# The first five of eight contraction chunks of an output projection, moved into a scan

## What is computed

```python
h = rms_norm(x, norm_mix_g[l])
p = h @ w_in[l]
...
o_att = memory_cross_attention(q, mem_n, w_mk[l], w_mv[l])
o_conv = conformer_conv(pc, conv_w[l], conv_b[l], conv_ln_g[l], conv_ln_b[l])
o_rwkv = rwkv7_bidirectional(pr, ...)
x = x + jnp.concatenate([o_att, o_conv, o_rwkv], axis=-1) @ w_out[l]
x = x + expert_choice_ffn(rms_norm(x, norm_ffn_g[l]), w_router[l], w_e_gate[l], w_e_up[l], w_e_down[l])
```

## Time and profile before

| what | us |
|---|---|
| median of 3 runs | 1869.56 |
| lowest and highest | 1868.42, 1872.74 |
| the profiled execution | 1867.28 |
| its span in the trace | 1865.3 |

### The profile page before, as it was taken

One profiled execution on the slowest core, in us unless ns is written; L12 is line 12 of the kernel. 1 busy time (PEld: TensorE's weight loads), 2 busy tenths in 40 slices (PEclk: granted clock), 3 DMA queues, 4 the chain that ended last, 5 costly groups with the idle time before them and its releaser, 6 DMA issues.

```text
span 1865.3 us, 25999 instructions
## 1 busy us (share of the span) xinstructions
PE 1476.8 (79%) x11135; PEld 844.7 (45%) x11135; DVE 418.2 (22%) x849; ACT 302.9 (16%) x671; POOL 118.1 (6%) x223
## 2 busy tenths in 40 slices
PE   6999988889896888888888859877857576765764
PEld 2845866768444443433433238666532132321311
DVE  1011225330016122212221253744330000000002
ACT  1101223540001111111111111432110010100100
POOL 3000022000000000000000002222000000000000
PEclk9999999898988899999999979887879898988988
DMA  9762362123484599999999962200329999999995
GB/s 352 163 257 81 114 245 96 46 90 113 180 297 158 227 428 429 428 428 428 431 428 428 396 246 92 83 3 3 138 100 412 429 428 429 428 429 428 429 428 231
DMA packets 86556, 512.05 MB, mean 275 GB/s; under 512 B 9783, under 2 KB 14168, under 8 KB 61910
## 3 DMA queue, kind: packets, MB, share of 16 engines
q1 hardware_dynamic: 82742, 501.95, 66.3%
q0 software_dynamic: 3744, 9.06, 2.1%
HBM read 506.10 MB, written 3.15 MB: 273 GB/s over the span
## 4 chain that ended last, share of the span: by engine, by line
PE 60%; DMA 24%; issue 6%; DVE 5%; ACT 3%; POOL 1%; SPq 1%; POOLq 0%; ACTq 0%; DVEq 0%; PEldq 0%
PE ps L1229 48%; DMA ring<-in_w_e_up 15%; DMA ring<-in_exp_w 7%; PE ps L1654 4%; PE ps L1828 3%; DMA ring<-in_ada_w 1%; DMA brow<-in_ada_b 1%; DVE arena L2457 1%; PE ps L1261 1%; PE ps L1639 1%; ACT arena L998 1%; DMA arena<-in_causal 1%; ACT arena L988 1%; DVE stats L2144 0%; PE ps L2097 0%
## 5 line engine op out<-in xcount | busy, mean ns | idle before, releaser
L1229 PE MATMUL ps<-ring,arena 128*32 128x512 f32 (+4 forms) x3572 | 481.8, 651 | 164.1 <-DMA ring<-in_w_e_up 92.1
L1229 PEld LDWEIGHTS ps<-ring,arena 128*32 128x32 f32 (+1 forms) x3572 | 137.0, 123 | 455.3 <-issue 387.1
L1229 PE MATMUL ps<-hTs,ring 128*128 128x256 f32 (+2 forms) x1120 | 250.7, 384 | 3.3 <-PE ps L1229 3.3
L1229 PEld LDWEIGHTS ps<-hTs,ring 128*128 128x128 f32 (+2 forms) x1120 | 211.5, 190 | 42.2 <-issue 11.1
L1229 PE MATMUL ps<-arena 128*128 (+5 forms) x576 | 140.1, 399 | 2.4 <-POOL arena L667 2.4
L1654 PE MATMUL ps<-arena 128*128 128x512 f32 x256 | 117.5, 601 | 29.0 <-DVE arena L2457 29.0
L1229 PEld LDWEIGHTS ps<-arena 128*128 128x128 f32 (+1 forms) x576 | 122.8, 292 | 19.7 <-issue 12.8
L1229 PE MATMUL ps<-ring,hTs 128*128 128x512 f32 (+2 forms) x288 | 103.7, 513 | 0.0
L1654 PEld LDWEIGHTS ps<-arena 128*128 128x128 f32 x256 | 46.0, 189 | 103.0 <-ACT arena L1000 57.1
L2457 DVE COPY arena<-ps 128x512 f32<-128x512 f32 x32 | 22.1, 692 | 251.6 <-PE ps L1229 251.6
L2744 DVE TENSOR_TENSOR arena<-arena,ps 64x512 f32<-64x512 f32 x16 | 11.0, 690 | 298.9 <-ACT arena L1184 298.9
(11 more groups left out here) (428 smaller groups left out, 1217.6 us busy)
## 6 DMA issues: line engine op xcount, KB each, us to landing
ring<-in_exp_w SPq DMA_DIRECT2D x96, 2048.0 KB, 18.8
ring<-in_w_e_gate SPq DMA_DIRECT2D x32, 2048.0 KB, 18.8
ring<-in_w_e_up SPq DMA_DIRECT2D x32, 2048.0 KB, 23.3
ring<-in_w_e_down SPq DMA_DIRECT2D x32, 2048.0 KB, 24.4
ring<-in_w_in SPq DMA_DIRECT2D x22, 2048.0 KB, 14.1
ring<-in_ada_w SPq DMA_DIRECT2D x12, 2048.0 KB, 12.8
ring<-in_w_out SPq DMA_DIRECT2D x4, 2048.0 KB, 12.1
ring<-in_w_br_hg SPq DMA_DIRECT2D x2, 2048.0 KB, 15.7
```

The lines of the kernel that those rows point to most:

```text
L1229: return nc.tensor.matmul(o, lhsT, rhs, start=start, stop=stop)
```

## The change

The products of chunks 0 to 4 are taken out of the tail and put in front of the levels of pair 1, into banks 1 and 2 of both directions. VectorE adds each of these four partial results to `x` within the levels, one in each level, after both transposes. `solved` of pair 1 waits until all four are added, since it writes the same banks. The Silu of the convolution moves between the pairs. In the tail only the products of chunks 5 to 7 remain, in the same four banks as before, and their four additions. No product is added or left out; four additions are.

```diff
@@ scalar engine, in the loop over pairs, behind the state copies
+                if p == 0:
+                    act.wait_ge(S("conv_normed"), 1)
+                    for c in range(3):
+                        ins = nc.scalar.activation(MIX[:, 2 + c, :], CV[:, c, :], ACT.Silu, bias=col(1, VB["cbb"] + c),
+                                                   scale=col(1, VB["cg"] + c))
+                    ins.then_inc(S("conv_ready"), 1)
...
@@ tensor engine, solved(p, d)
                 pe.wait_ge(S("prod_out"), 8 * p + 6 + d + 1)
+                if p:
+                    pe.wait_ge(S("early_out"), 4)
...
@@ tensor engine
+            wout2 = [tile("wout2") for _ in range(2)]
+
+            def early_out(i, t):
+                return dbank(t, 1 + i, 0, 512)
+
+            def project_early():
+
+                for i in range(2):
+                    is_out(pe, jM(f"O{i}"))
+                pe.wait_ge(S("conv_ready"), 1)
+                for d in range(2):
+                    pe.wait_ge(S("prod_out"), 14 + d + 1)
+                for i in range(2):
+                    for t in range(TT):
+                        for k in range(5):
+                            ins = mm(early_out(i, t), MIX[:, k, t * P:(t + 1) * P], slot(wout2[i], (8, 512))[:, k, :],
+                                     k == 0, k == 4)
+                        ins.then_inc(S("early_full"), 1)
...
                     pe.wait_ge(S("prod_out"), 8 * p + 2 + 2 * d + 2)
+                if p:
+                    project_early()
                 with pe.Fori(0, 4) as lev:
...
-            for i in range(2):
-                is_out(pe, jM(f"O{i}"))
-            project(0, 1)
             pe.wait_ge(S("gn_squares"), 1)
+            outs = [(wout2[i], [job("y2", 2 * i + t) for t in range(TT)]) for i in range(2)]
             block_sums("gn2", c3(3072))
-            pe.wait_ge(S("conv_ready"), 1)
-            project(1, 5)
             pe.wait_ge(S("mix_ready"), 1)
-            project(5, KC)
+            for n, js in outs:
+                for t, j in enumerate(js):
+                    for k in range(5, KC):
+                        ins = mm(bank(j), MIX[:, k, t * P:(t + 1) * P], slot(n, (8, 512))[:, k, :], k == 5, k == 7)
+                    fills(ins, j)
...
@@ vector engine, in the loop over levels
                         nc.vector.transpose(XT[d], X[d]).then_inc(S("lev_out"), 1)
+                    if p:
+                        i, t = lev // 2, lev % 2
+                        dve.wait_ge(S("early_full"), lev + 1)
+                        c = slice(512 * i, 512 * i + 512)
+                        tt(x[:, t, c], x[:, t, c], dbank(t, 1 + i, 0, 512), ALU.add).then_inc(S("early_out"), 1)
```

More of the change, by code:

```diff
@@ L2700, in _ @@
             say(tt(MIX[:, 5:8, :], YY, BON, ALU.add), "mix_ready")
+            dve.wait_ge(S("early_out"), 4)
             for i in range(4):
```

## The result

| | kernel before | changed kernel |
|---|---|---|
| median of 10 runs, us | 1869.77 | 1882.99 |
| lowest and highest | 1866.51, 1875.02 | 1878.67, 1889.95 |
| the profiled execution, and its span | 1867.28, 1865.3 | 1887.13, 1884.8 |

The ratio is 1.0069, with a 95% interval of 1.0052 to 1.0086: the change costs 12.9 us, 9.7 to 16.1. The runs of either kernel spread over 8 to 11 us, which is new: the three runs shown ahead of the prediction lay within 4.3.

A forecast was written before the change was run, and what follows sets the result against it. It took TensorE's chain to bound pair 1 of the scan and VectorE's chain to `mix_ready` to hold the tail. Scan +16.8 and tail -2.5 gave +14.3, so a median of 1883.9 us, range 1875.5 to 1889.

The forecast's parts named there:

- 17.3 for the long products: Pair 1 of the scan, before the levels: forty passes lie whole on TensorE's chain, adding 17.3 us.
- 3.8 for two gaps: Pair 1's levels: the instruction gaps of 1.34 and 2.47 us go, as packets arrive during the long passes; 3.8 us saved.
- 1.5 for the clock in the levels: Pair 1's levels: TensorE at full clock after 17 us of dense work; 1.5 us saved.
- 0.8 for three additions: Pair 1's levels: three additions on VectorE each delay the next level by 0.27 us; 0.8 us added.
- 1.3 for the fourth: End of pair 1's levels: `solved` waits for the fourth addition behind the second transpose; 1.3 us added.
- 2.7 for the packets behind the loop: `solved` to the steps: forty more pairs shift packet boundaries, so the steps begin at 19.9 against 16.7 us; 2.7 later.
- 0 for the Silu: Between the pairs: pair 1's copies end 2.3 us later, covered by an existing gap; 0, or 1.8 without that cover.
- -2.5 for the tail: Tail: ends 2.5 us earlier, with TensorE idle 9.5 us, then its first 5 us at half clock.
- the signs named: Trace marks expected, among them `y_done` near 1337, five or more gaps between `solved` and the steps, TensorE idle 9 us.
- The one by which packets run ahead: Scan: long products let packets run far ahead, the four later gaps vanish; 12.4 us less, 1871.5, no change; chance 0.06.
- The rival in which the packets cost nothing and the clock is kind: Scan and tail: no packet cost, 2.5 less in the tail, last steps up to 2.8 less; 1875.9; chance 0.17.
- The rival with a bad clock: Clock falls during the long products (1887.3), and also stays low for all tail passes (both 1895); chance 0.15.

The follow-up runs named there:

- the long products alone: Kernel before plus the twenty early products in front of pair 1's levels, results dropped, tail, Silu and additions unchanged; 1.0059, +11.0 us (7.1 to 15.0).
- twenty tiny products: Kernel before plus twenty 32x32 by 32x8 products, results dropped, where the change has its long ones; 0.9998, -0.4 us.
- sixty-four tiny products: Kernel before plus sixty-four 32x32 by 32x8 products (128 pairs, one packet), results dropped, ahead of pair 1's levels; 1.0031, +5.8 us.
- the Silu alone: Kernel before with only the Silu of the convolution moved between the pairs; 1.0007, +1.3 us (-1.9 to +4.5).
- the tail alone: Kernel before with the products of chunks 0 to 4 left out of the tail and computed nowhere else; 0.9985, -2.8 us (-5.8 to +0.4).
- the additions moved: Changed kernel with the first three additions made while TensorE runs the long products and the fourth in level 0; 1.0073 against the kernel before.
- chunk 0 early: Kernel before with only chunk 0's four products early, additions ahead of the levels and in level 0, Silu at its old place; 1.0008, +1.5 us.

## Why the prediction was right

It gave 1883.9 (1875.5 to 1889); the median is 1882.99, and the measured difference 12.9 against 14.3. The mechanism is shown by two kernels that take the change apart: the long products alone cost 11.0 in the scan (7.1 to 15.0), and taking them out of the tail gives back 2.8 (-0.4 to 5.8). The small terms are less sure, and that the sum came so close is in part luck: some were too large, one too small. Point by point:

- **17.3 for the long products**: 17.41, at full clock, in one piece. Shown by the trace and by the products alone (+11.0 net of what they buy back, where 14.7 was forecast).
- **3.8 for two gaps**: gone in the changed kernel; in the list of waits no gap over 0.2 lies between 1297.69 and 1309.
- **1.5 for the clock in the levels**: full clock in all four, each 2.9, and so in all five kernels with twenty long products; right. That it is they who keep the clock up is likely, but the levels at full clock differ without them too: one of four before, two of four behind twenty tiny products.
- **0.8 for three additions, 1.3 for the fourth**: 0.2 and 1.3. The first term was mis-sized: of a delay of 0.43 I took 0.15 as hidden, and it was nearly all.
- **2.7 for the packets behind the loop**: that the boundaries move is shown (twenty against sixty-four tiny products), the size was wrong: 0.9 in the one pair of traces at equal clock, and within what kernels with the same boundaries differ by. I had the second packet land 4.7 us behind `solved` with a wait; no wait stood there, and there were four gaps ahead of the steps where the prediction said five or more. In the kernels with the changed alignment the last packet arrived 17.9 to 19.3 behind `solved`, not 19.9, against 19.1 to 20.2 in three of the four with the old one, whose steps are then already under way (the fourth, with the Silu alone, shows no such wait).
- **0 for the Silu**: about 0.5 in the changed kernel's trace. The cover by the gap was there, but not whole, and it was that good only because `turned` ran at half clock there; by the traces it would be 1.3 to 1.8 at the clock that the prediction's own rows had.
- **-2.5 for the tail**: -2.6 with the tail alone and -2.3 with the additions moved, as forecast with 5 us of half clock (24 passes in 12.13 and 13.04). In the profiled execution of the changed kernel it was -0.4, since the clock was low from 1324 on and both block sums took twice as long (2.90 and 2.93 against 1.53 and 1.46). That is a matter of the execution, not of the change: other executions show it with the kernel's tail unchanged (33.38 and 33.41 with sixty-four tiny products and with the Silu alone, `gn1` at half clock). Against those, its 30.01 is 3.4 less.

With the sizes as measured the sum is 17.4 - 3.8 - 1.5 + 0.2 + 1.3 + 0.9 + 0.5 - 2.5 = +12.5, beside 12.9 (9.7 to 16.1) by the ratio. The interval holds the 14.3 as well, so the time can't tell which of the two sums is better. Of the signs named, `y_done` came near 1340, not 1337; the difference lies ahead of the long products, which began at 1280.29 where 1277.36 was taken.

**The rivals.** The one by which packets run ahead needed the gaps behind the loop to vanish. They were all there, in each of the five kernels with twenty long products, after 17 us in which the queue had nothing else to do, so little more than one packet was held ahead. The Trainium skill, "Runtime: NRT & Kernel Launch", section "Instruction fetch mechanics", says that the next page is fetched while the current one executes, which fits; that crossing a boundary is mostly hidden does not, with four gaps of 0.95 to 2.48 here. The rival in which the packets cost nothing and the clock is kind gave 1875.9, under the lowest run (1878.67): its first half may be true, but 24 passes took 12.13 to 13.22 in every tail that had the idle time, and the steps took 9.98 in the changed kernel, as long as the 9.89 before (7.91 to 9.66 in the other four with twenty long products). The rival with a bad clock came in by halves: the clock fell at the start of the products in the kernel with them alone (18.74 instead of 17.41), not in the changed kernel. The two profiled executions differ by 19.9, 7.0 more than the 12.9. Three places where the same work took longer make 6.8 of it: pair 0 (+2.7), the first 48 passes of `solved` (2.79, 1.51 in pair 0: +1.3) and the two sums of the tail (+2.8). That this is the account of it was not shown, as other stretches differ too.

## What to carry to other kernels

Work that fills another engine's wait is paid for by that wait; moved to a place where its own engine is the chain, it costs its full length, and the old place gives back only what stuck out beyond the wait. So before moving a block, mark in the timeline which of its passes lie under the other engine's work (here eleven products of twenty behind the second sums, and the four ahead of them, which hold `mix_ready` up by 0.85) and move at most the rest. Gaps in the supply of instructions are a landing place where long instructions cost little (in the trace with chunk 0 early they were gone), though no version here gained by it. And keep an engine's side work away from the last step of a loop, where the next one waits for it: that addition cost 1.3, the three ahead of it 0.06 each.

## What the runs showed of the hardware

- Small fp32 products of 32 or 64 rows outrun the supply of instructions. Each 128 pairs of weight load and matmul end in a gap, and the resumptions lie 3.5 to 4.0 us apart (before: 1301.56, 1305.02, 1309.02, 1313.02; 128 matmuls in each stretch between two of them, of which TensorE is busy for 1.5 to 3.6 us). The pattern returns when exactly 128 pairs are added and shifts when 40 are.
- A loop body of 192 pairs runs without any packet being moved once its packets are in (before, 0 GB/s from 1286 to 1294; in the changed kernel from 1302 to 1310).
- The same instructions in the same place take different times from one execution to the next, with the granted clock of TensorE low in other stretches: pair 0 took 47.58 to 50.49 us in twelve traces (its last steps at 0.80 in the window of 1266 to 1268 before, at 0.50 in that of the changed kernel). The Trainium skill, "TensorE: Matmul & The Clock Gate", section "What's actually happening", has it that the low clock is the default and activity lifts it; the traces agree in that the clock fell to 0.50 within 9.55 us of idleness in the tail and was back some 5 us into the 24 passes (the rows with the additions moved).
- Terms under 2 us could not be seen in the time at 6 to 12 runs a kernel, but could in the stretches of the traces.
